# Moving the stationary operands of a two-layer block relative to the weight ring in SBUF

## The reference, cut to what matters

```python
h = rmsnorm(x, attn_norm_g)
z = h @ w_in                                   # 2048 -> 5200
...                                            # pool mixer, index scores, top-64 attention
x = x + jnp.concatenate([y_pool, y_attn], axis=-1) @ w_out
x = x + conv_ffn(rmsnorm(x, ffn_norm_g), w_up, conv_w, conv_b, w_down)   # 2048 -> 11264, 5632 -> 2048
# second layer: w_in_2, two attentions, w_branch_a_2, w_branch_b_2, w_out_2,
h = h + (jax.nn.silu(hn @ w_gate[l]) * (hn @ w_up[l])) @ w_down[l]
return rmsnorm_2(h, final_norm)
```

## Time and profile before

| | us |
|---|---|
| median of 3 runs | 2439.99 (2439.48 to 2440.35) |
| the profiled execution, its own time | 2440.54 |
| its span, first to last instruction | 2438.7 |
| TensorE matmuls busy | 2423.8 (99%) |
| TensorE weight loads busy | 2014.8 (83%) |
| VectorE busy | 1319.6 (54%) |
| ScalarE busy | 1181.1 (48%) |
| GpSimd busy | 58.4 (2%) |

### The profile page before, as it was taken

How to read it: one execution, slowest core, us unless ns; L and a number is a source line. 1 busy time by engine, 2 the same in 40 slices (tenths; PEclk the granted TensorE clock), 3 DMA queues, 4 the chain that set the end, 5 groups by cost and what they waited for, 6 DMA issues and landing times.

```text
span 2438.7 us, 29829 instructions
## 1 busy us (share of the span) xinstructions
PE 2423.8 (99%) x11152; PEld 2014.8 (83%) x11152; DVE 1319.6 (54%) x1480; ACT 1181.1 (48%) x1489; POOL 58.4 (2%) x97
## 2 busy tenths in 40 slices
PE   9999999999999999999999999999999999999998
PEld 7788888888888888888888888888888888888886
DVE  5775456666666655445454554665545445454443
ACT  5545445555555544445455544544444444444443
POOL 0000000000000000001120000000000000000000
PEclk9999999999999999999999999999999999999999
DMA  7665456666666655556655556556666666666664
GB/s 248 179 175 165 150 186 182 189 184 186 187 184 183 187 190 190 190 191 186 186 168 171 161 163 182 188 184 189 188 190 185 190 191 186 190 192 207 193 193 144
DMA packets 240905, 449.38 MB, mean 184 GB/s; under 512 B 20085, under 2 KB 26965, under 8 KB 240689
## 3 DMA queue, kind: packets, MB, share of 16 engines
q1 hardware_dynamic: 239952, 445.83, 60.8%
q0 software_dynamic: 624, 2.24, 0.3%
q10 hardware_dynamic: 240, 0.11, 0.0%
HBM read 446.02 MB, written 2.10 MB: 184 GB/s over the span
## 4 chain that ended last, share of the span: by engine, by line
PE 70%; issue 29%; DMA 0%; DVE 0%; ACT 0%; SPq 0%; POOLq 0%; POOL 0%; DVEq 0%; ACTq 0%
PE acc L553 22%; PE acc L555 22%; PE acc L554 21%; PE bank L544 2%; PE bank L706 1%; PE bank L734 0%; DMA w_raw<-in_w_in 0%; PE bank L764 0%; PE bank L683 0%; PE bank L735 0%; PE bank L709 0%; PE bank L749 0%; DVE w_lo L1268 0%; ACT w_hi L943 0%; PE acc L582 0%
## 5 line engine op out<-in xcount | busy, mean ns | idle before, releaser
L1268 DVE TENSOR_TENSOR w_lo<-w_raw,w_hi 128x1024 fp32r<-128x1024 f32 (+1 forms) x843 | 1029.6, 1222 | 1079.6 <-ACT w_hi L943 1078.4
L943 ACT ACTIVATE w_hi<-w_raw 128x1024 fp32r<-128x1024 f32 (+1 forms) x843 | 890.2, 1056 | 1217.1 <-PE acc L555 1210.0
L553 PE MATMUL acc<-w_hi,xT_hi 128*128 128x512 f32 x2236 | 878.9, 393 | 0.3 <-DVE w_lo L1268 0.3
L555 PE MATMUL acc<-w_hi,xT_lo 128*128 128x512 f32 x2236 | 868.9, 389 | 0.0
L554 PE MATMUL acc<-w_lo,xT_hi 128*128 128x512 f32 x2236 | 867.7, 388 | 0.0
L555 PEld LDWEIGHTS acc<-w_hi,xT_lo 128*128 128x128 f32 x2236 | 419.6, 188 | 87.5
L553 PEld LDWEIGHTS acc<-w_hi,xT_hi 128*128 128x128 f32 x2236 | 419.9, 188 | 85.5 <-issue 1.8
L554 PEld LDWEIGHTS acc<-w_lo,xT_hi 128*128 128x128 f32 x2236 | 420.1, 188 | 83.3
L553 PE MATMUL acc<-w_hi,f_hi 128*128 128x512 f32 x704 | 274.3, 390 | 0.0
L555 PE MATMUL acc<-w_hi,f_lo 128*128 128x512 f32 x704 | 273.9, 389 | 0.0
L554 PE MATMUL acc<-w_lo,f_hi 128*128 128x512 f32 x704 | 273.9, 389 | 0.0
(11 more groups left out here) (203 smaller groups left out, 1178.1 us busy)
## 6 DMA issues: line engine op xcount, KB each, us to landing
w_raw<-in_w_up SPq DMA_DIRECT2D x264, 512.0 KB, 3.6
w_raw<-in_w_in SPq DMA_DIRECT2D x199, 512.0 KB, 3.6
w_raw<-in_w_down SPq DMA_DIRECT2D x176, 512.0 KB, 3.7
w_raw<-in_w_gate SPq DMA_DIRECT2D x88, 512.0 KB, 3.6
w_raw<-in_w_out SPq DMA_DIRECT2D x64, 512.0 KB, 3.7
w_raw<-in_w_branch_a SPq DMA_DIRECT2D x16, 512.0 KB, 3.9
w_raw<-in_w_branch_b SPq DMA_DIRECT2D x16, 512.0 KB, 3.9
w_raw<-in_w_in SPq DMA_DIRECT2D x10, 320.0 KB, 3.0
```

The source lines that it names most:

```text
L553: pe.matmul(o, l, w_hi[:, slot, k, 0:width], start=start, stop=False)
L555: last = pe.matmul(o, m, w_hi[:, slot, k, 0:width], start=False, stop=stop)
L943: act.activation(in_slot(w_hi, slot, width), in_slot(w_raw, slot, width), ACT.Copy).then_inc(w_split_hi, 1)
L1268: dve.tensor_tensor(in_slot(w_lo, slot, width), in_slot(w_raw, slot, width), in_slot(w_hi, slot, width).bitcast(F32), ALU.subtract).then_i ...
```

## The change

The three edits are unused tiles. `place_x` shrinks from 384 to 128 bytes, which moves `x_res`, `xT_hi` and `xT_lo` down by 256 bytes; `place_ring` adds these 256 bytes in front of `w_raw`, so the ring and all that follows it up to `place_inner` keep their addresses; `place_inner` grows from 64 to 128 bytes, which moves all that lies behind it up by 64 bytes. No instruction, wait, transfer or size changes.

```diff
-        sb("place_x", [P, 96])
+        sb("place_x", [P, 32])
         x = sb("x_res", [P, NT, D])
         xT_hi, xT_lo = sb("xT_hi", [P, KT, S], F32R), sb("xT_lo", [P, KT, S], F32R)
+        sb("place_ring", [P, 64])
         w_raw = sb("w_raw", [P, RING, KC, CW])
...
-        sb("place_inner", [P, 16])
+        sb("place_inner", [P, 32])
         with ExitStack() as r:
             y_hi, y_lo = sb("y_hi", [P, KT, S], F32R, r), sb("y_lo", [P, KT, S], F32R, r)
```

## The result

The changed kernel takes 2461.95 us (median of 4 runs, 2461.2 to 2463.84), the kernel before 2439.73 us on the same chip (median of 4): +22.2 us, ratio 1.0091, 95% interval 1.0079 to 1.0103. The profiled execution took 2461.2 us, its span 2459.4 us.

What follows compares the result with a forecast made beforehand. TensorE's streaming pace, 226.7 ns a matmul, was taken to bound the kernel. Span 2438.7 plus 1.8 around it, plus 10.2, gave 2450.7 us, stated as 2450 since the median lies 0.55 lower; range 2424 to 2464 us.

Steps and rivals of the forecast that it cites:

- surcharge of 13.3 ns: Time per 512-column TensorE matmul beyond its columns: 226.7 ns between starts against 213.3, 133 us over 9996 matmuls.
- The vector engines, the ring, the transposes at nothing: Splits, vector work on x, y and f, and transposes costed at nothing; 1210.0 us of waiting covers splits and vector work.
- `xT` at 256 costs 0: The 6612 matmuls with xT, moved to distance 256 from the stationary tile, taken as like 0: 0 ns each.
- The faster rival: The xT stream gains at 256: 2 ns less for 6612 matmuls, -13.2 us, 2427 us; chance 0.28.
- the slower-still one: Rival that xT at 256 also runs at the unsettled 231.3 ns: 2440 + 30 + 10 = 2480 us; chance 0.10.
- the kw row for 256: kw group, 80-column loads from the ring while xT moves: durations at distance 256 average 277.3 ns, lowest of three.
- I take 3 ns: Price for each of the 3384 matmuls with f, y, m, cq and ckv at distance 64: +10.2 us.
- the forecast's own range: Range for the forecast case, y, f and m dearer with xT unmoved: 2446 to 2456 us, chance 0.33.
- the wide one: The range for the whole kernel's time said to hold 8 in 10: 2424 to 2464 us.
- The kw rows' +1.3 ns: kw group's distance 64 against 256, for 80-column loads; scaled by 128 / 80 to 2.1 ns, +7.1 us.
- unsettled pace of 231.3 ns: Eight matmuls behind a burst of transposes, 4.6 ns above the settled pace; upper bound of +15.6 us at 64.
- interlock: Settled 226.7 ns held likely to be a favourable meeting of the two SBUF reads that a 64-byte shift spoils.

Runs made afterwards that it cites:

- x256: Kernel before with only the edits ahead of the ring: x_res and xT at 256 bytes from the ring, the rest at 0; 2440.05 us, ratio 1.0000.
- y64: Kernel before with only the edit ahead of y: y, m, cq, ckv and f at 64 bytes from the ring, x at 0; 2461.83 us, ratio 1.0088.
- widths64: As y64, but the w_down_2 groups stream 256, 320, 384 and 448 of 512 columns; 113.3 ns a matmul at 256, 202.2 at 448.
- widths0: Same cut stream widths in w_down_2 as widths64, but with f at distance 0; 120.0 ns a matmul at 256 columns, 206.7 at 448.
- the curve at 512: Six kernels against the one before, only unused tiles resized, other distances on xT and on y, m, cq, ckv, f; 2471.74 to 2505.84 us.
- x240_f16: Against the kernel before, xT cut to lie 16 bytes below a multiple of 256 and f 16 above, y and m at 0; 2456.24 us, ratio 1.0070.

## Why the prediction was right or wrong

- That TensorE's pace bounds the kernel and the surcharge of 13.3 ns is what an address can act on: right. The time grew by what TensorE's starts with `f`, `y`, `m`, `cq` and `ckv` moved apart, and ScalarE's wait grew with it.
- The vector engines, the ring, the transposes at nothing: right, their busy times are unchanged within 0.2 us.
- `xT` at 256 costs 0: right, and `x256` shows it alone (ratio 1.0000). The faster rival and the slower-still one both fall. The reason given, that the kw row for 256 was the lowest, was weak, as the next points show.
- `f`, `y`, `m`, `cq`, `ckv` are the ones that pay: right, and `y64` shows it alone.
- The step that failed is the term "I take 3 ns": it measures 6.67 ns. The sum was +10.2 us for 22.2, the forecast's own range ended at 2456, and the time of 2461.95 lay only in the wide one. Two choices made it small. The kw rows' +1.3 ns was the mean of three durations each, out of a group that scatters from 274 to 282 ns, and it was scaled by the load's columns (128 / 80). But kw streams 256 columns, where another order of the distances holds: `widths64` and `widths0` have 64 cheaper than 0 at 256 columns (113.3 against 120.0 ns, with loads of 128), and the curve at 512 puts 192 far below 64, kw above it. Such a row can't be carried over to 512 columns by any factor. And the unsettled pace of 231.3 ns was taken as the upper bound. It is an average over intervals on the way to a settled pace, while a stream can settle on a pace worse than it (233.3, and 234.3 at 96). The idea written beside it, that the settled 226.7 is an interlock which 64 bytes spoil, agrees with the runs, but even the 4.6 ns of that bound would have made only 15.6 us. The sign that was named, `f` above 226.7 and `xT` unmoved, came true; twelve matmuls with `f` take 2.80 us, not 2.76, and those of the two down projections together 13.9 us more, not 6.
- The rule of the Trainium skill ("TensorE: Matmul & The Clock Gate", "Step-by-step: what each phase is for") that loading the next weights takes no SBUF read bandwidth from the running matmul would have had 0. Here stationary tiles 64 bytes further from the moving ones cost 6.67 ns a matmul and the same tiles moved together with them cost none. That the two reads get in each other's way inside SBUF is the simplest reading of this, but it was only argued: what a run shows is the dependence on the distance.

What stays open is the mechanism: why the period is 256 bytes, why a half load is no cheaper at distance 0, why 256 and 448 columns turn the order around, and what picks the pace where one distance has two.

## What to carry to other kernels

Where TensorE streams without a gap and loads a new stationary tile for each matmul in fp32r, the distance in bytes between the stationary and the moving tiles, modulo 256, is a setting of its own: here it moved the whole kernel by up to 2.7%, and a small tile declared ahead of the big ones is enough to change it. At 512 columns and loads of 128, keep both at the same place modulo 256. If the width of the stream or the load is another, measure again, since the price of a distance holds for one pair of widths alone: at 256 and 448 columns 64 bytes apart was the better place. Read the pace from starts many matmuls apart, as a busy time of 99% hides all of this, and read it in more than one stretch, as the first stretch of `x240_f16` alone would give 228.3 ns for what is 226.7 in nearly half of them.

## What the runs showed of the hardware that wasn't expected

Behind a burst a stream settles within some ten matmuls and keeps its pace to the end of the stretch. Which one depends on the distance modulo 256 (226.7 to 234.3 ns at 512 columns, surcharges of 13.3 to 21.0 ns) and, at some distances, on the stretch: 226.7 or 228.3 ns at 240, 226.7 or 233.3 at 16. A load of 64 columns instead of 128, at distance 0, went with a pace of 229.8 ns instead of 226.7. And at 256 and 448 columns 64 bytes apart is faster than 0, by 6.7 and 4.5 ns a matmul.
